# Normalised rows turned before their gains: the start of a hybrid encoder block on one core

## The reference

```python
def rms_norm(x, gain):
    y = xf * lax.rsqrt(jnp.mean(xf * xf, axis=-1, keepdims=True) + EPS)
    return y * gain

h = rms_norm(x, norm_mix[l])
proj = h @ w_in[l]          # all branches: attention, state space, memory attention, gates
...
x = x + merged @ w_out[l]
x = x + moe_ffn(rms_norm(x, norm_ffn[l]), ...)   # 32 experts, top 4
```

## Time and profile before

| | us |
|---|---|
| median of 3 runs | 1453.02 (1452.72 to 1453.64) |
| the profiled execution | 1452.76 |
| its span | 1450.6 |
| PE busy | 1426.2 |
| DVE busy | 587.3 |
| ACT busy | 405.6 |
| POOL busy | 63.2 |

### The profile page before, as it was taken

How to read it: one execution, slowest core, us unless ns; L and a number is a source line. 1 busy time by engine, 2 the same in 40 slices (tenths; PEclk the granted TensorE clock), 3 DMA queues, 4 the chain that set the end, 5 groups by cost and what they waited for, 6 DMA issues and landing times.

```text
span 1450.6 us, 18622 instructions
## 1 busy us (share of the span) xinstructions
PE 1426.2 (98%) x7575; PEld 820.9 (57%) x7575; DVE 587.3 (40%) x1149; ACT 405.6 (28%) x601; POOL 63.2 (4%) x50
## 2 busy tenths in 40 slices
PE   6999999999999999999999999999999999999998
PEld 6898888877788864444444444444444444433433
DVE  5779788677788651211111121121212111111111
ACT  5766666556644531101010110101011011101100
POOL 5120000111100000000000000000000000000000
PEclk9999999999999999999999999999999999999999
DMA  7455444654573979999999999999999999999997
GB/s 253 141 187 176 158 144 151 209 164 160 174 269 130 381 282 422 430 427 427 427 430 428 427 427 430 429 427 428 429 429 428 428 429 428 427 428 429 429 426 295
DMA packets 74000, 491.27 MB, mean 339 GB/s; under 512 B 5264, under 2 KB 8976, under 8 KB 49376
## 3 DMA queue, kind: packets, MB, share of 16 engines
q1 hardware_dynamic: 71280, 487.57, 83.1%
q10 hardware_dynamic: 2160, 2.62, 0.6%
q0 software_dynamic: 512, 0.43, 0.1%
HBM read 488.93 MB, written 1.07 MB: 338 GB/s over the span
## 4 chain that ended last, share of the span: by engine, by line
PE 82%; DMA 9%; DVE 5%; ACT 2%; issue 1%; DVEq 0%; ACTq 0%; SPq 0%
PE ps L1930 26%; PE ps L1968 13%; PE ps L1591 8%; PE ps L1593 8%; PE ps L1592 8%; PE ps L1858 7%; DMA regions<-in_w_gate 6%; PE ps L1578 4%; PE ps L1910 4%; DMA regions<-in_w_up 3%; DVE regions L1166 2%; DVE splits L1020 1%; PE ps L1805 1%; PE ps L1938 1%; ACT splits L707 1%
## 5 line engine op out<-in xcount | busy, mean ns | idle before, releaser
L1930 PE MATMUL ps<-regions,sig 128*64 128x512 f32 x2048 | 463.3, 594 | 4.1 <-DMA regions<-in_w_gate 3.8
L1930 PEld LDWEIGHTS ps<-regions,sig 128*64 128x64 f32 x2048 | 141.7, 137 | 276.7 <-issue 260.1
L1968 PE MATMUL ps<-regions,tmp 128*64 128x512 f32 x1024 | 225.1, 592 | 0.0
L1591 PE MATMUL ps<-splits,regions_r 128*128 128x512 f32 x512 | 205.9, 402 | 0.1
L1593 PE MATMUL ps<-splits,regions_r 128*128 128x512 f32 x512 | 200.1, 391 | 0.0
L1592 PE MATMUL ps<-splits,regions_r 128*128 128x512 f32 x512 | 199.8, 390 | 0.0
L707 ACT ACTIVATE splits<-halves 128x1024 fp32r<-128x1024 f32 x152 | 159.1, 1056 | 95.9 <-PE ps L1593 81.0
L1020 DVE TENSOR_TENSOR splits<-halves,splits 128x1024 fp32r<-128x1024 f32 x132 | 161.1, 1224 | 43.5 <-ACT splits L707 42.2
L893 ACT ACTIVATE work<-work 128x512 f32<-128x512 f32 x32 | 20.1, 629 | 474.9 <-DVE work L1518 474.9
L1968 PEld LDWEIGHTS ps<-regions,tmp 128*64 128x64 f32 x1024 | 71.7, 137 | 132.0 <-issue 129.6
L1858 PEld LDWEIGHTS ps<-craw,regions 128*128 128x128 f32 x1024 | 119.2, 192 | 25.6 <-issue 25.2
(11 more groups left out here) (299 smaller groups left out, 1188.4 us busy)
## 6 DMA issues: line engine op xcount, KB each, us to landing
regions<-in_w_gate SPq DMA_DIRECT2D x64, 2048.0 KB, 29.1
regions<-in_w_up SPq DMA_DIRECT2D x64, 2048.0 KB, 27.4
regions<-in_w_down SPq DMA_DIRECT2D x64, 2048.0 KB, 30.2
halves<-in_w_in SPq DMA_DIRECT2D x48, 1024.0 KB, 5.1
halves<-in_w_br_b SPq DMA_DIRECT2D x8, 1024.0 KB, 5.0
halves<-in_w_mem_kv SPq DMA_DIRECT2D x8, 1024.0 KB, 5.0
halves<-in_w_br_a SPq DMA_DIRECT2D x4, 1024.0 KB, 5.2
halves<-in_w_br_c SPq DMA_DIRECT2D x4, 1024.0 KB, 7.5
```

Source lines behind the costliest of these rows:

```text
L1591: pe.matmul(out, lhs[0], rhs[0], start=start, stop=False, skip_group_check=True)
L1930: last = pe.matmul(ps[64 * h:64 * h + 64, bank, :], xgT[:, 4 * k + c], eslots[slot][:, c, h * NB:(h + 1) * NB], start=(k == 0 and c == 0), ...
L1968: last = pe.matmul(ps[64 * h:64 * h + 64, D_BANK, :], actT[:, c, 64 * k:64 * k + 64], eslots[slot][:, c, h * NB:(h + 1) * NB], start=False ...
```

## The change

The rows are scaled by their root alone (a tensor_scalar). The gains come as eight rows of 128 numbers into a corner of the gates' buffer `sig`; PE turns them once, DVE copies them to a column for each 128 channels (`gain1_sb`), and `hT` joins `yT` and `memT` in the table `TURNED`: two activations with a scale on ACT and two scalar_tensor_tensors on DVE for each pair, where one plain operation on each stood. PE turns the blocks of a pair by rows of tokens and waits for each row block by itself. In the list of steps pairs 2 and 3 move behind product 0 and product 1. On POOL the four `shade` tables move ahead of the 15 small DMAs.

```diff
-    s = [("split", 0), ("split", 1), ("rest", 0), ("hT", 0), ("rest", 1), ("hT", 1), ("hT", 2), ("hT", 3),
-         ("split", 2), ("rest", 2)]
+    s = [("split", 0), ("split", 1), ("rest", 0), ("hT", 0), ("rest", 1), ("hT", 1), ("split", 2), ("rest", 2)]
     for w in range(UNITS):
         s.append(("gemm", name, i, w % QUARTERS, w))
+        if w < 2:
+            s.append(("hT", w + 2))
...
-        gain1 = S[:, 3, 0:D]
+        gain1_rows, gain1_sb = sig[0:KC, 0, T:T + P], sig[:, 1, 0:KC]
+        TURNED = {"yT": (ybT, gssm_sb), "memT": (memT, gmem_sb), "hT": (hT, gain1_sb)}
...
-            sp.dma_start(gain1, g_mix.partition_broadcast(P)).then_inc(sem("gain_landed"), 16)
+            sp.dma_start(gain1_rows, g_mix.rearrange("(c p) -> c p", p=P)).then_inc(sem("gain_landed"), 16)
...
             # ACT
-                elif kind in ("yT", "memT"):
-                    if step[1] == 0:
+                elif kind in TURNED:
+                    pair, gain = TURNED[kind]
+                    if step[1] == 0 and kind == "hT":
+                        act.wait_ge(sem("gain_ready"), 1)
+                    elif step[1] == 0:
                         act.wait_ge(sem("small_landed"), 16 * 12)
...
             # DVE
+            dve.wait_ge(sem("gain_turned"), 1)
+            dve.tensor_copy(gain1_sb, ps[:, EXP_BANK, 0:KC]).then_inc(sem("gain_ready"), 1)
             dve.wait_ge(sem("row_squares"), 2)
             rstd(rs_x, ss_x, D)
-            dve.wait_ge(sem("gain_landed"), 16)
             for t in range(TT):
-                dve.scalar_tensor_tensor(out=xn[:, t], in0=x_in[:, t], scalar=rs_x[:, t:t + 1], in1=gain1,
-                                         op0=ALU.mult, op1=ALU.mult).then_inc(sem("rows_scaled"), 1)
+                dve.tensor_scalar(xn[:, t], x_in[:, t], rs_x[:, t:t + 1], None, ALU.mult).then_inc(sem("rows_scaled"), 1)
...
             # PE
+            pe.wait_ge(sem("gain_landed"), 16)
+            pe.transpose(ps[:, EXP_BANK, 0:KC], gain1_rows, ident[0:KC, 0:KC]).then_inc(sem("gain_turned"), 1)
...
+                elif kind == "hT":
+                    b = group()
+                    for t in range(TT):
+                        pe.wait_ge(sem("rows_scaled"), t + 1)
+                        for j in range(2):
+                            c = 2 * step[1] + j
+                            last = turn(ps[:, b, j * T + t * P:j * T + (t + 1) * P], xn[:, t, c * P:(c + 1) * P])
+                    last.then_inc(misc_ready, 1)
```

More of the change, by code:

```diff
@@ L629, in _ @@
             pool.memset(craw[:], 0.0).then_inc(sem("craw_zero"), 1)
+            ones_pairs = ones.rearrange("p (k b) -> p k b", b=2)
+            for half in range(2):
+                at0 = 64 * (1 - half)
+                pool.affine_select(out=shade[:, 2 * half], in_=ones, compare_op=ALU.is_gt, fill=0.0, base=-2 * at0,
+                                   pattern=[[-1, P]], channel_multiplier=2).then_inc(sem("shades"), 1)
+                pool.affine_select(out=shade[:, 2 * half + 1].rearrange("p (k b) -> p k b", b=2), in_=ones_pairs,
+                                   compare_op=ALU.is_equal, fill=0.0, base=at0, pattern=[[1, P // 2], [0, 2]],
+                                   channel_multiplier=-1).then_inc(sem("shades"), 1)
             pool.dma_start(rel_raw, rel_rev).then_inc(sem("rel_landed"), 16)
@@ L647, in _ @@
                            norm_ffn.rearrange("(h p c) -> p h c", h=2, p=P)).then_inc(gain2_landed, 16)
[L648 to L655, removed]
             for step in SCHED:
@@ L707, in _ @@
                     act.activation(hi, raw, ACT.Copy).then_inc(hi_ready, 1)
-                elif kind in ("yT", "memT"):
-                    pair, gain = (ybT, gssm_sb) if kind == "yT" else (memT, gmem_sb)
-                    if step[1] == 0:
+                elif kind in TURNED:
[3 more added lines that the diff above has]
+                    elif step[1] == 0:
                         act.wait_ge(sem("small_landed"), 16 * 12)
@@ L718, in _ @@
                                            scale=gain[:, c:c + 1]).then_inc(sem(kind + "_rounded"), 1)
-                elif kind in ("hT", "mergedT"):
+                elif kind == "mergedT":
                     for k in range(MISC_GROUPS[kind]):
@@ L723, in _ @@
                         act.wait_ge(misc_ready, n_misc + 1)
[L724 removed]
+                        act.activation(mergedT[0][:, 2 * c2:2 * c2 + 2],
                                        ps[:, MISC_BANKS[n_misc % 3], :].rearrange("p (c t) -> p c t", c=2), ACT.Copy)\
@@ L988, in _ @@
                 kind = step[0]
-                if kind in ("yT", "memT"):
-                    pair, gain = (ybT, gssm_sb) if kind == "yT" else (memT, gmem_sb)
+                if kind in TURNED:
+                    pair, gain = TURNED[kind]
                     for k in range(MISC_GROUPS[kind]):
@@ L1005, in _ @@
                                 ins.then_inc(misc_taken, 1)
-                elif kind in ("hT", "mergedT"):
-                    both = hT if kind == "hT" else mergedT
+                elif kind == "mergedT":
+                    both = mergedT
                     for k in range(MISC_GROUPS[kind]):
@@ L1605, in _ @@
                 kind = step[0]
-                if kind in ("memT", "hT"):
-                    if kind == "memT":
-                        pe.wait_ge(sem("mem_landed"), 16)
-                    else:
-                        pe.wait_ge(sem("rows_scaled"), 2)
-                    src = mem_sb if kind == "memT" else xn
-                    by_columns(lambda t: src[:, t], step[1])
+                if kind == "memT":
+                    pe.wait_ge(sem("mem_landed"), 16)
+                    by_columns(lambda t: mem_sb[:, t], step[1])
+                elif kind == "hT":
[6 more added lines that the diff above has]
+                    last.then_inc(misc_ready, 1)
                 elif kind == "gemm":
```

1 line of the change is left out of this document (removed).

## The result

The changed kernel took 1454.93 us (median of 20 runs, 1454.51 to 1456.96), the one before 1452.79 in the same measurement (1451.8 to 1453.64). The ratio, taken from the means of the runs, is 1.0016, with a 95% interval of 1.001 to 1.0022. By the medians it is 2.1 us slower, beyond the end of the range forecast (1454.3) and with the other sign. The profiled execution of after took 1454.51 for a span of 1452.3 (before 1452.76 and 1450.6).

A forecast was written before the change was run, and what follows sets the result against it. PE bounds the kernel, busy 1426 of 1450.6 us. Product 3 was to end at 13.7 + 11.52 + 0.88 + 1.1 = 27.2 against 28.45, giving 1453.02 - 1.2 = 1451.8 us, range 1450.4 to 1454.3.

The forecast's parts named there:

- What bounds, and the carry: Whole kernel: PE is the bound, and a microsecond won or lost by the first products counts one for one at the end.
- Gains and landing: SP's loads: without the 512 KB broadcast the first weight half lands at 9.7 instead of 11.56; the 4 KB cost zero.
- weights landed + 4.0: Start of product 0: 13.7 from weights landed at 9.7, with a range of 13.4 to 14.35.
- Rows, 0.71 each: DVE's scaling of two rows at the start: 0.71 each against 1.26, ending at 10.9 rather than 11.98.
- Rival (3): DVE's row scaling waits for POOL's DMA issues (0.76 each), rows end at 12.4, about 1453.1; chance 0.09.
- the path by halves: Pair 0's rounding before product 0: 0.84 on ACT, DVE 0.10 later, 1.00 on DVE, 0.14 to PE.
- the start and its slow part: Products 0 to 3: start 13.7, slow matmuls cost 1.1 against 0.83, end 27.2 against 28.45, 1.2 us sooner.
- rival (1): PE's clock rise stays at 18.0, so products start sooner but slow: 0.5 us sooner, 1452.5; chance 0.20.
- the three readings offered for the moment: PE's clock rise: 5.9 us after the first turn (16.2), still at 18.0, or 1.9 us after the first product.
- Queues behind the moved pairs: ACT, POOL and DVE up to dt's turn: later work, constants ending at 30.0, still ready at 32.8 for PE's 33.0.
- the narrowest place: DVE's copy of dt, ready at 32.8 and wanted at 33.0: slack 0.2 us, no wait taken, can cost 0.3.
- Rival (4): DVE's copy of dt comes after PE wants it, losing 0.3 of the gain: 1452.1; chance 0.08.

The follow-up runs named there:

- e3: Kernel before with only the new order of steps (pairs 2 and 3 turned behind products 0 and 1): 1456.47 us, 1.0027.
- e9: e8 with the sums of DVE's constants moved ahead of the variance: 1452.33 us, 0.9997 against the kernel before.
- e10: Changed kernel with POOL's four affine selects back behind its 15 small DMAs: 1455.78 us, 1.0019 against the kernel before.
- e4: Changed kernel with the old order of steps, all four pairs turned before product 0: 1452.15 us, 0.9997 against the kernel before.
- e1: Changed kernel with weight unit 7's low part on DVE instead of POOL: 1454.22 us, 1.001 against the kernel before.
- e2: Changed kernel with DVE's constants made earlier (sums before the variance, tensor_scalars behind low part 2): 1452.9 us, 1.0001 against the kernel before.
- e5: Changed kernel with POOL's low part of unit 7 held back until DVE's constants are done: 1455.08 us, 1.0017 against the kernel before.
- e11: Changed kernel once more, unchanged, for a second profile: 1455.13 us, 1.0018 against the kernel before.
- e7: e2 with 22 unused mask matmuls on idle PE, 10 ahead of the gains' turn and 12 behind it: 1452.78 us, 1.0 against the kernel before.
- e12: e7 with eight more mask matmuls in the gap before product 0: 1451.89 us, 0.9993 against the kernel before.
- e8: e4 with 22 unused mask matmuls, 10 and 12 around the gains' turn: 1451.05 us, 0.999 against the kernel before.
- e6: Kernel before with 30 unused mask matmuls at the start of PE's queue, ahead of the turns: 1451.67 us, 0.9995.

## Why the prediction failed

**What bounds, and the carry: right.** The loss arose in the first 40 us, and a microsecond at dt's turn was one at the expert start and, within 0.9 us in most rows of the table, one at the end (e3 and e9 are off by more).

**Gains and landing: the sign right, the size wrong, without effect.** The first split was at 8.55, sooner than the bound of 9.45 from the queue's interval. By "weights landed + 4.0" product 0 would have begun at 12.5. It began at 14.05: ACT was through with the splits at 10.5 and waited for pair 0's turns, which the sum had put ahead of it. The 4 KB of gains landed at 6.2, inside the bounds taken, and cost nothing.

**Rows, 0.71 each: 0.88 here.** The estimate from 128 and 256 elements is met in e10, where POOL issues small DMAs; beside the issue of `wr_sb` it was 0.17 more for each. Rival (3) had POOL's issues as a cause, at less than a quarter of its price in this place. Pair 0 reached ACT at 11.95, where 11.6 was forecast. From there the path by halves was as told, 2.1 us for 2.08, so product 0 began at 14.05 for 13.7.

**The first failing step, the start and its slow part: rival (1).** The last matmul of product 3 began at 28.12, before at 28.21: 0.1 us sooner where 1.2 was forecast. Three things took the rest. The sum counted the products of before from 16.10, the end of the last turn; the first of them began at 15.74, so 0.36 less could be won. Product 0 began 0.35 later than forecast. And the fast spacing came at 18.03, as before, not at 16.2: eight more matmuls were slow, 0.74, where the sum had 1.1 - 0.83 = 0.27, so another 0.47. None of the three readings offered for the moment holds in all runs: from PE's first turn it was 5.9 us before, 7.8 in after, 6.1 in e4 and some 9 in e10; from the first product 2.3, 4.0, 1.6 and some 5.5. Before and e4, where the turns run into product 0, have the short times behind the first product; where a gap of 1.2 to 1.4 us lies in front of it (after, e1, e2, e3, e5, e10, e11) it was 3.3 to 5.5. The forecast had that gap and gave it no part in the clock. That the gap is the reason is not shown. After, e1, e2 and e5 run the same turns and products on PE up to there and changed at 18.0, 18.9, 18.2 and 18.6: the moment isn't fixed by the program.

On the rule of the Trainium skill (TensorE: Matmul & The Clock Gate, Part 4) that transposes don't count, the products alone would have set the moment. The spread from 1.6 to 5.5 us behind the first of them doesn't fit that as the only condition, and doesn't refute the rule.

**The step that made the loss: "Queues behind the moved pairs".** The first step took the gain away; this one turned the sign. The forecast placed DVE's block of constants from about 24.6 to 30.0, and gave it 5.4 us, read from a stretch in which POOL was idle. The order of the queues was as told, everything in it 1.1 us later, as PE was too: low part 4 at 24.54, the block from 25.68, and without the meeting its end would be 31.1, so 5.4 was right for a free DVE. But POOL starts its low part of unit 7 when ACT has split that unit, at 29.57, and moves with the products, while the block had moved by 3.5 us. That the two now overlap could be worked out from the earlier trace rows and POOL's timeline of before, with the block moved; the forecast put no term for it. It named this the narrowest place, with 0.2 us of slack, and allowed 0.3; the meeting took 2.2 and PE waited 2.0. The slack of 0.2 is what lies between these two. Rival (4) had the place and PE's wait, at a seventh of the price; rival (3) had the exclusion of DVE and POOL, in another place and with the DMA issues only. Neither put both together.

The Trainium skill's rule (SBUF — State Buffer, Who interferes with whom), that tensor_scalar and copy in their two-port modes and GpSimd block each other, agrees with what happened at 29.52: 0.29 became 2.47, the length of POOL's 2.38. The prediction had set it aside because a COPY ran free beside a DMA issue and because another row was only lengthened. Rows of before that it doesn't use already had the full effect (timelines of DVE and POOL, before):

```profile
31.72 0.69 DVE L1190 COPY regions<-regions 16x256 f32<-16x256 f32 x1
```
```profile
29.67 2.60 POOL L662 TENSOR_TENSOR splits<-halves,splits 128x1024 fp32r<-128x1024 f32 x1 [8.46 <-ACT splits L707]
```

The COPY that reads PSUM (L1221, 31.38) runs in its usual 0.41 beside POOL; the one that reads SBUF takes 0.69, to just behind POOL's end at 32.27, and 0.27 where POOL is done (35.93 in after).

**Is the cause shown?** That the meeting costs the 2 us is: the order alone brings it (e3), e1 removes it with the block of constants in its place and the wait is gone, e2 removes it and with it the whole loss, e5 moves it and the loss stays. That the moved pairs bring nothing at the start is shown by the profiles of e2 (expert start -0.1) and e3 (PE 0.56 late before it waits); the median of e2 (+0.2 us, interval -1.2 to +1.5) agrees but is too wide to show it. Not settled are what sets the moment of the clock's rise, and why the medians differ from the expert starts by up to 1.6 us, each of which comes from one profile.

## What to carry to other kernels

A step that is put behind others moves every later block of its engines' queues: for each DVE block list what GpSimd does at its new time, for one tensor_scalar of four columns can wait for a whole 2.4 us operation there. Time won at the very start, where PE runs at the lower clock level, is in part given back (0.74 of 1.69 us here) unless the clock is brought up by work on the idle PE; that work may have to cover the gaps too (e7 against e12). And a step with 0.2 us of slack behind a long sum has none.

## What the runs showed of the hardware

- **Who waits is not who has the earlier record.** DVE's row begins at 29.52 and POOL's at 29.57, and DVE waits; in e3 it is 30.22 and 30.23; in e5 31.41 and 31.45, where DVE's goes first and POOL's record is a microsecond longer. An operation holds to its end: two low parts of DVE, 2.36 by themselves, take 4.40 to 4.57 where an operation of POOL goes ahead of one of them (e4, e5, e8, e9). Where POOL's comes behind both, before, DVE keeps its 2.36 and POOL's record is 2.60.
- **DMA issues on POOL and DVE's tensor_scalars lengthen each other, by less than a whole operation.** Two rows of 1024 take 1.76 in after, beside the issue of `wr_sb` (1.04, before 0.93), and 1.42 in e10, beside two issues of `head_rows` (0.89 and 0.67, before 0.57 each). No run has these rows with POOL idle.
- **The gap after warming up.** e7 lost the upper level in an idle time of 1.76 us in front of product 0; e6 kept it through one of 2.46, e8 through 1.24. Nor does it help to leave the turns out: between the last mask matmul and product 0 lie 4.4 us in e7, 5.1 in e6 and 4.9 in e8. What tells them apart is open.
- **A small load in front moves the queue by more than its bytes.** With 4 KB in place of the 512 KB broadcast the next load landed 3.0 us sooner, where its bytes at the 429 GB/s of the earlier trace rows are 1.2. POOL's later DMAs have little part in it: with them as early as before the first split begins at 8.69 (e10), with the broadcast kept at 11.53 (e3).
